# Gate projections by seven products of half blocks in a hybrid decoder layer, with tokens and gates parked in DRAM

## The reference

```python
h = rms_norm(x, norm1_g)
q, k, v, u, vs, ga, gb = split(h @ w_in)           # 512, 128, 128, 512, 512, 1024, 1024 columns
u  = gelu(u);  vs = layer_norm(gelu(vs))
oa = attention(q, k, v)                            # sliding window with sinks, 512 wide
ob = u * (causal_spatial(w_spatial) @ vs + b)      # 512 wide
h2 = sigmoid(ga) * (oa @ w_branch_a) + sigmoid(gb) * (ob @ w_branch_b)
x  = x + h2 @ w_out
x  = x + hier_moe(rms_norm(x, norm2_g))            # 16 experts of 256, top 2 of one group
```

## Time and profile before

| | |
|---|---|
| median of 3 runs | 940.69 us (940.2 to 943.37) |
| the profiled execution | 940.68 us, of which 938.9 us are the span of the trace |
| PE busy | 902.6 us (96%) |
| DVE, ACT, POOL busy | 459.1, 357.7, 226.6 us |
| mean DMA rate over the span | 126 GB/s |

### The profile page before, as it was taken

One profiled execution on the slowest core, in us unless ns is written; L12 is line 12 of the kernel. 1 busy time (PEld: TensorE's weight loads), 2 busy tenths in 40 slices (PEclk: granted clock), 3 DMA queues, 4 the chain that ended last, 5 costly groups with the idle time before them and its releaser, 6 DMA issues. The chain is left out here.

```text
span 938.9 us, 16170 instructions
## 1 busy us (share of the span) xinstructions
PE 902.6 (96%) x5389; PEld 808.4 (86%) x5390; DVE 459.1 (49%) x828; ACT 357.7 (38%) x623; POOL 226.6 (24%) x242
## 2 busy tenths in 40 slices
PE   8999999999999999999999999999889999999994
PEld 7777776787999999999999999999788888888883
DVE  5677876433222222222222236543887768577561
ACT  5666655210232112111121132221536667577561
POOL 2434221345220000000000011000043356354562
PEclk9999999999999999999999999999899999999998
DMA  7321310200302201101001006874539898989833
GB/s 248 113 68 47 123 51 22 72 0 1 104 1 68 68 34 42 59 34 66 34 34 67 22 25 208 315 263 124 176 102 305 289 321 275 320 261 314 276 54 45
DMA packets 57359, 118.57 MB, mean 126 GB/s; under 512 B 7469, under 2 KB 32749, under 8 KB 57296
## 3 DMA queue, kind: packets, MB, share of 16 engines
q1 hardware_dynamic: 49824, 100.10, 30.8%
q0 software_dynamic: 7488, 17.85, 8.5%
HBM read 105.37 MB, written 23.00 MB: 137 GB/s over the span
## 5 line engine op out<-in xcount | busy, mean ns | idle before, releaser
L1408 ACT ACTIVATE gate<-psum 128x352 f32<-128x352 f32 x48 | 22.4, 466 | 209.9 <-PE psum L79 209.7
L77 PE MATMUL psum<-w_hi,hT_hi 128*128 128x512 f32 (+3 forms) x224 | 83.0, 370 | 3.6 <-issue 1.9
L2193 DVE TENSOR_TENSOR hT_lo<-room,hT_hi (+1 forms) x32 | 72.1, 2291 | 17.2 <-ACT hT_hi L1881 17.2
L77 PE MATMUL psum<-hT_hi,x_xT_hi 128*128 (+1 forms) x192 | 77.8, 405 | 1.4 <-DVE x_xT_lo L2348 0.8
L78 PE MATMUL psum<-w_lo,hT_hi 128*128 128x512 f32 (+3 forms) x224 | 78.9, 352 | 0.0
L79 PE MATMUL psum<-w_hi,hT_lo 128*128 128x512 f32 (+3 forms) x224 | 78.8, 352 | 0.0
L77 PE MATMUL psum<-hT_hi,w_hi 128*128 128x352 f32 x240 | 77.4, 323 | 0.0
L78 PE MATMUL psum<-hT_lo,w_hi 128*128 128x352 f32 x240 | 76.9, 321 | 0.0
L79 PE MATMUL psum<-hT_hi,w_lo 128*128 128x352 f32 x240 | 76.9, 320 | 0.0
L78 PE MATMUL psum<-hT_lo,x_xT_hi 128*128 (+1 forms) x192 | 75.7, 394 | 0.0
L79 PE MATMUL psum<-hT_hi,x_xT_lo 128*128 (+1 forms) x192 | 75.6, 394 | 0.0
(11 more groups left out here) (353 smaller groups left out, 2306.3 us busy)
## 6 DMA issues: line engine op xcount, KB each, us to landing
room<-in_w_gu SPq DMA_DIRECT2D x16, 2048.0 KB
dn_raw<-in_w_dn SPq DMA_DIRECT2D x16, 1024.0 KB
g_w_raw<-in_w_ab SPq DMA_DIRECT2D x15, 768.0 KB, 4.3
xT_chunk<-in_xT SPq DMA_DIRECT2D x8, 528.0 KB, 3.7
x_in<-in_x SPq DMA_DIRECT2D x8, 512.0 KB, 3.5
out_y<-y SPq DMA_DIRECT2D x8, 512.0 KB, 3.4
hn_rows<-squares SPq DMA_DIRECT2D x8, 512.0 KB, 3.2
o_w_raw<-in_w_out_t SPq DMA_DIRECT2D x7, 512.0 KB, 6.8
```

The costliest lines, as they stand in the source:

```text
L77: eng.matmul(out, lh, rh, start=first and k == 0, stop=False)
L1408: act.activation(gate[:, (ab + c) % 2, :], bank(psum, gate_pair(ab, c))[:, 0:TC], ACT.Sigmoid).then_inc(gated.sem, 1)
L2193: dve.tensor_tensor(gu_lo[:, buf, ks], gu_raw[:, buf, ks], gu_hi[:, buf, ks].bitcast(F32), ALU.subtract).then_inc(gu_lo_made.sem, 1)
```

## The change

The two block programs `sgu_gate_phase` and `gates_phase` become one, `dense_phase`, whose loops are all written out.

**Gates.** Features are cut in two halves (k), tokens in two halves of 528 (HALF, taken as two pieces HC of 264), and output columns in two halves; a turn takes 128 columns of each half of the columns of one gate. Where eight block products of four chunks each stood, seven stand, of sums of blocks: A are blocks of weights, S1 to S4 sums of them, B blocks of h, T1 to T4 sums of those. There are eight turns, and 56 products of 24 matmuls of 264 columns. Their results are added by DVE out of PSUM in a chain (e1, u2, u3, out), and the sigmoids of the four blocks of the result are written by ACT in place and stored to DRAM.

**Sums of tokens.** `attention_phase` stores each scaled tile of h to DRAM, and h_scale waits until the store of the tile before has landed. It also stores oaT at its end, since the sums T1 and T2 take its place. In the opening the tokens come back as blocks, and DVE makes the sums and their low parts, ACT their high parts.

**u.** The last quarter of u is taken in four pieces of 264 columns, the far tokens first. The low half of ob is made by DVE (`ob_low`) and no longer by POOL. **Branches.** After all gates come the sixteen branch products (b, then a), with oaT and the sigmoids loaded back; POOL adds the two branches, and all eight chunks of h2 are split in this block. The first 18 matmuls of the output product (FIRST_K = 2 chunks) stand at the end of this block too.

```diff
@@ attention_phase, SP and DVE
+            def store_h(t):
+                sp.wait_ge(h_scaled, 2 * (t + 1))
+                sp.dma_start(io["h"][:, :, toks(t)], h_raw[:, :, :, 0:rows(t)]...).then_inc(h_stored, DMA)
+            store_h(0)
             for t in range(2, NT):
                 load_x(t)
                 load_xT(t)
+                if t >= 3:
+                    store_h(t - 2)
...
+            sp.wait_ge(oa_lo_made, NT)
+            for o, name in zip(oaT, ("oa_hi", "oa_lo")):
+                sp.dma_start(io[name], o[:, :, :]...).then_inc(oa_stored, DMA)
...
                 dve.wait_ge(h_lo_made, 2 * t)
+                dve.wait_ge(h_stored, DMA * t)
@@ dense_phase
+    UNITS = [(q, slice(c * TC, (c + 1) * TC)) for q in range(KE - 1) for c in range(3)]
+    UNITS += [(KE - 1, slice(c * HC, (c + 1) * HC)) for c in (2, 3, 0, 1)]
+    SUMS = ("A11", "S2", "S3", "A12", "S1", "A22", "S4")
+    SLOTS = 5
+        MOVING = (quarter(0, 0), T[2], T[3], quarter(1, 0), T[1], T[4], quarter(1, 1))
+        X_BANKS = (0, 1, 5, 6, 7, 2, 3, 4)
...
+        def _(sp):
+            load_u(1)
+            load_tokens(0, T_raw[1], 0, 1)
+            load_tokens(1, T_lent[3], 1, 1)
+            load_tokens(2, T_lent[1], 0, 0)
+            load_u(2)
             for used in keep["used"]:
                 sp.sem_clear(used)
...
+        def _(pool):
+            for v in range(KD, BRANCHES - 1):
+                pool.wait_ge(multiplied, 3 * v + 3)
+                pool.tensor_tensor(here, here, part[v % 2], ALU.add).then_inc(h2_summed, 1)
...
+        def _(act):
+            def gates(g):
+                n, i = divmod(g, len(SUMS))
+                for c in range(2):
+                    if i == 0:
+                        act.activation(e1[:, c], x_of(g, c), ACT.Copy).then_inc(e1_made, 1)
+                    elif i >= SUMS.index("A12"):
+                        act.wait_ge(x_taken, taken(g, c))
+                        act.activation(ready, ready, ACT.Sigmoid).then_inc(sg_made, 1)
...
+            for g in range(GATES):
+                gates(g)
+                if g in (0, 1):
+                    t_high(4, g)
+                high(g + SLOTS - 1)
...
+        def _(pe):
+            def gate_product(g):
+                pe.wait_ge(w_hi, g + 1)
+                pe.wait_ge(w_lo, g + 1)
+                for c in range(2):
+                    pe.wait_ge(x_taken, taken(g - 4, c))          # from g = 4 on
+                    product(pe, x_of(g, c), ..., KH).then_inc(m_made, 1)
...
+        def _(dve):
+            for u in range(US):
+                if u in (0, 3, 6):
+                    u_low(u // 3 + 1)
+                u_step(u)                                         # ob_low(u - 1), then the product with mixT
+                if u in (1, 2):
+                    first_sums(u - 1)
+                if u in (3, 4):
+                    second_sum(u - 3)
+                if u in (5, 6, 7):
+                    n = (1, 3, 2)[u - 5]
+                    for piece in range(2):
+                        t_low(n, piece)
+                if u == US - 4:
+                    low(0)
+                if u == US - 3:
+                    for name in ("S1", "S2", "S3"):
+                        weight_sum(0, name)
+                if u == US - 2:
+                    low(1)
+                    fourth_sum(0)
+            low(2)
+            ob_low(US - 1)
+            low(3)
+            fourth_sum(1)
+            weight_sum(0, "S4")
+            for g in range(GATES):
+                gates(g)
+                if g in (0, 1):
+                    t_low(4, g)
+                elif n + 1 < TURNS:
+                    for name in {2: ("S1",), 3: ("S2", "S3"), 4: ("S4",)}.get(i, ()):
+                        weight_sum(n + 1, name)
+                low(g + SLOTS - 1)
```

More of the change, by code:

```diff
@@ L37 @@
 TC = NTOK // 3
-EARLY = ((0,), (1,), ())
-LATE = sum(len(ks) for ks in EARLY)
+HALF = NTOK // 2
+HC = HALF // 2
+FIRST_K = 2
+ARENA = SG * NTOK + 4 * KD * P + 2 * (KD // 2) * HALF + 4 * TC + 2 * (KD // 2) * P
 NG, EPG = 4, 4
@@ L93, in u_bank @@
     return bank(psum, 2 + c)
-def gate_pair(ab, c):
-    return 2 * ((3 * ab + c) % 4)
 class Step:
@@ L310, in _ @@
             load_xT(1)
+            def store_h(t):
+                sp.wait_ge(h_scaled, 2 * (t + 1))
+                sp.dma_start(io["h"][:, :, toks(t)], h_raw[:, :, :, 0:rows(t)].rearrange("p a k c -> p (a k) c")).then_inc(h_stored, DMA)
+            store_h(0)
             for t in range(2, NT):
@@ L326, in _ @@
             load_vs(1)
+            store_h(PT - 1)
             sp.wait_ge(h_scaled, 2 * NT)
             sp.dma_start(kT_cache[:, :], io["cache_kT"]).then_inc(k_cache_in, DMA)
+            store_h(PT)
             sp.wait_ge(h_lo_made, 2 * NT)
+            sp.wait_ge(h_stored, DMA * NT)
             load_vs(3)
@@ L362, in _ @@
             sp.wait_ge(vs_stored, DMA)
+            sp.wait_ge(oa_stored, 2 * DMA)
         @block.gpsimd
@@ L1520, in merge_moe_phase @@
     hT, ident, y = (keep["hT_hi"], keep["hT_lo"]), keep["ident"], keep["y"]
-    h2 = keep["h2"]
     gu_flat, dn_raw = keep["gu_raw"], keep["dn_raw"]
@@ L1872, in keep_y @@
                 ins.then_inc(y_copied, 1)
-            for k in range(LATE, KD):
-                act.activation(hT[0][:, k, :], h2[:, k, :], ACT.Copy).then_inc(h2_hi, 1)
             for f in (gu_hi_made, dn_hi_made, xT_hi_made, silu_made, hidT_hi_made, out_made):
@@ L2023, in logits_turn @@
                 mm.then_inc(lg_turned, 1)
-            for k in range(KD):
-                wait(pe, h2_lo, k - LATE + 1)
+            for k in range(FIRST_K, KD):
                 for c in range(3):
-                    mm = term(0, c, k, k == 0, k == KD - 1)
+                    mm = term(0, c, k, False, k == KD - 1)
                     if k == KD - 1:
@@ L2197, in _ @@
                 f.begin(dve)
-            for k in range(LATE, KD):
-                dve.wait_ge(h2_hi, k - LATE + 1)
-                dve.tensor_tensor(hT[1][:, k, :], h2[:, k, :], hT[0][:, k, :].bitcast(F32), ALU.subtract).then_inc(h2_lo, 1)
             dve.memset(y[:, PT, :], 0.0).then_inc(zeroed, 1)
+            weights(1)
             dve.wait_ge(const_in, DMA * 4)
             dve.tensor_tensor(w_r, w_r, g2[:, :].unsqueeze(2).broadcast_to([P, KD, NR]), ALU.mult).then_inc(w_r_made, 1)
-            weights(1)
             dve.wait_ge(made, 3)
@@ L2429, in hybrid_layer @@
         with ExitStack() as dense:
+            with ExitStack() as short:
+                for name in ("hT_hi", "hT_lo"):
+                    keep[name + "_raw"] = sb(short, name + "_raw", [P, KD, NTOK])
             for name in ("hT_hi", "hT_lo"):
@@ L2432, in hybrid_layer @@
             with ExitStack() as branches:
+                with ExitStack() as short:
+                    for name in ("oaT_hi", "oaT_lo"):
+                        keep[name + "_raw"] = sb(short, name + "_raw", [P, KE * NTOK])
                 for name in ("oaT_hi", "oaT_lo"):
```

706 lines of the change are left out of this document (423 added, 283 removed).

## The result

The changed kernel takes **924.82 us** in the median (924.2 to 926.06, four runs), the kernel before beside it 940.6 us (940.2 to 943.37, four runs): a ratio of 0.9828, with a 95% interval of 0.9806 to 0.985. Faster, by 15.8 us, as forecast; 928.7 us had been predicted, within 924 to 934, so the time lies 0.8 us above the range's lower end. The span of its profiled execution is 923.6 us, against 938.9.

The account below looks back on a forecast made before the run. PE, at work 96% of the span, was taken as the bound. 23.9 us gained less 11.9 given back takes the 938.9 us span to 926.9; with execution's extra 1.8 that is 928.7 us, range 924 to 934.

Parts of the forecast that it names:

- The matrix work, -17.8: PE's matmuls from u to the output product: 320.5 us before, 302.8 after, with 264 columns 122.8 ns apart.
- Rival 4: Narrow matmuls don't pay: at 136 ns or more for 264 columns the gates gain nothing, 947 us; chance 0.03.
- rival 5: The change doesn't do what it says: halves refetched or PE's written-out code arriving late, 942 us; chance 0.04.
- The gates in their steady state, nothing: Gate turns: 19 us of DVE and ACT chain hidden beside 20.6 us of PE, costed at nothing.
- rival 1: Gates: the round DVE, ACT, DVE outlasts PE's 2.95 us a product; 948 us at 3.3 us; chance 0.13.
- The opening, 4.6 and 1.5 for the clock: First gate products: PE waits 4.6 us for DVE's low parts, plus 1.5 us for one lowered clock.
- The opening's loads: Block start: u weights and token blocks land in time at 390 GB/s, so PE doesn't wait for them.
- Attention, 2.4: h_scale of tile 2 waits for tile 1's store, landing at 33.6 us; 2.4 us lost, bounds 0.5 and 5.
- Branches, 0.5: Branch products: DVE beside POOL's adds lags by 3.5 us at most, costing PE 0.5 us.
- The end, 1.3 and 1.6 for the clock: Block's end: PE idles 1.3 us behind DVE's 4.1 us tail, and the lowered clock costs 1.6 us as before.
- Rival 2: The opening costs nothing: DVE and ACT keep up and no clock falls, 922.6 us; chance 0.14.

Follow-up runs that it names:

- the run in quarters: The kernel before with its gated feed-forward in four pieces of 264 columns in place of three of 352, all eight products kept: 946.58 us, ratio 1.0066.

## Why the prediction came out as it did

The mechanism was right: PE's work fell, PE waited in the opening but not in the turns, and attention lost by its store. Two groups of terms were mis-sized, of opposite sign, and part of the nearness in time is luck. By the predicted sum the stretch between the marks would have been 302.8 + 9.5 = 312.3 us; it was 305.1, so 7.2 better. Attention was 2.8 worse, the block's start and what follows the block 1.0. 926.9 - 7.2 + 2.8 + 1.0 = 923.5; the span is 923.6. Of the 7.2, the spacing gave 1.7, the opening 4.4, the branches 0.2 and the end 1.8, together 8.1. About 1.0 us of the stretch is neither matmuls at their spacing nor one of the three idle places; such a rest of 0.8 us stood there before too, and the prediction had counted it as gained.

- **The matrix work, -17.8.** With 121.6 ns at 264 columns in place of 122.8 it is 1,440 x 0.0012 = 1.7 more, -19.5 us. The line through the two measured widths was right to 1%. Rival 4 is refuted by it, and for rival 5 nothing speaks: no idle place in the block is one in which PE's own instructions came late. The rule of the Trainium skill, "TensorE: Matmul & The Clock Gate", section "Back-to-back issue gap", by an estimate from whose figures this change would have lost nearly 6 us, doesn't agree with these fp32r matmuls: neither here nor in the run in quarters did narrower ones come at its spacing.
- **The gates in their steady state, nothing.** Right. In 300 to 450 us PE is busy all the time, and no wait stands in turns two to seven. In that stretch DVE waits 24.6 us for PE (33 times) and 29.9 for ACT's high parts (30 times, mostly 1.01 us). The tripled low parts show that rival 1's mechanism exists, and that its margin was about 0.9 us a product, more than the 0.25 us that the sum had left (2.7 against 2.95).
- **The opening, 4.6 and 1.5 for the clock.** 1.68 us, with the clock at 1.00 behind. The step that failed is the walk along DVE. DVE's timeline before the wait:

```profile
285.38 2.08 DVE L1630 TENSOR_TENSOR arena<-arena 128x512 f32<-128x512 f32 x3
287.38 0.43 DVE L1588 TENSOR_TENSOR w_lo<-arena,w_hi 128x264 fp32r<-128x264 f32 x1
287.73 0.43 DVE L1583 TENSOR_TENSOR arena<-arena,mixT 128x264 f32<-128x264 f32 x1
289.17 0.69 DVE L1640 TENSOR_TENSOR w_lo<-arena,w_hi 128x512 fp32r<-128x512 f32 x1 [1.01 <-ACT w_hi L1443]
289.78 1.25 DVE L1618 TENSOR_TENSOR hT_lo_raw<-hT_hi_raw,oaT_hi 128x1056 f32<-128x1056 f32 x1
...
294.02 0.69 DVE L1640 TENSOR_TENSOR arena_rounded<-arena,arena_rounded 128x512 fp32r<-128x512 f32 x1 [1.01 <-ACT arena_rounded L1443]
```

  An instruction of DVE shown as 0.43 us is followed by the next after 0.35 (287.38 to 287.73), one of 0.69 after 0.61 (289.17 to 289.78): their ends overlap the next start by 0.08 us, when nothing is waited for. I had added up the durations. Over the more than twenty DVE instructions of the opening that follow another at once, that is close to 2 us. A handover took less too, 0.03 us (DVE's product ends at 288.16, ACT starts at 288.19; ACT ends at 289.14, DVE starts at 289.17), and I had taken 0.1. No run separates the two. The effect: low(1), forecast 1.9 us late, ended at 289.86 as PE came for it, and low(2) (294.02 + 0.69 = 294.71) was 1.7 late instead of a further 2.4 behind. The page names ACT's w_hi as the releaser; the time of the wait's end shows that it was this low part. Moving a sum behind it moved the wait whole, which fits that it is the sum of DVE's and ACT's work up to there. POOL's share in it was as costed: with it back, 0.6 us, and 1.01 us in place of 0.52, as in the earlier trace rows.
- **The opening's loads.** No wait of PE, as walked.
- **Attention, 2.4.** 5.24. The chain of waits was the one forecast (store, h_scale, exponentials, L754); only the landing was wrong, 35.9 in place of 33.6. Of that, 0.7 us is my choice: the sum gave 34.3, and no row supports the step down to 33.6. For the rest, I had taken 390 GB/s from the earlier trace rows, a stretch of weight loads; among attention's own DMAs it was 205 to 344, and the next load of x joined at 32.16. To this came the clock, 0.54 for 3 us behind 3.83 us of idling, which I had costed in the opening and at the end but not here. The kernels with the store ahead of the loads start the block at 237.7 us in the mean, as before the change: the order was the whole loss. (5.24 is one execution's; with the same order the others lost 3.6 to 6.1.)
- **Branches, 0.5.** PE lost 0.30 us there, but by another way: the store of c22, not POOL beside DVE. POOL's adds took 3.40 us beside DVE, as the 2.9 and the contention suggest, and DVE's products out of PSUM stayed at 0.53, while low parts of 512 columns took 2.95 in place of 0.69; the lag never reached PE. What the Trainium skill says in "SBUF — State Buffer", section "Who interferes with whom", agrees with this trace: 1.93 us for one DVE sum with two SBUF inputs beside POOL's add (541.54), 0.52 without.
- **The end, 1.3 and 1.6 for the clock.** 1.06, and no fall of the clock. Windows of PE behind both idle places:

```profile
294.00:297.00 3.00, 2.19 (x18) 1.00 0.00 0
297.00:300.00 3.00, 3.00 (x27) 1.00 0.00 0
548.00:551.00 3.00, 2.32 (x15) 1.00 0.46 93
551.00:553.00 2.00, 2.00 (x15) 1.00 0.99 386
```

  I had carried the 1.5 us from an idle place of 2.08 us to shorter ones. In the runs with a longer tail the clock fell at this place, behind 2.74 and 6.09 us.

Rival 2 (the opening costs nothing, 922.6) came close in time, but not in its cause: the opening still cost 1.7 us, and attention cost more.

## What to carry to other kernels

When a chain on VectorE is walked to see who comes late, use distances between starts of busy neighbours, not durations; 0.08 us each adds up to the wait in dispute. When a change adds a wait for a store, look first at what stands ahead of the store in its DMA queue: here the place of one store cost about 5 us of a gain of 21, and no engine's busy time shows it. Fewer matmuls at a narrower width are worth the difference of counts times spacing at each width, and both spacings are to be read from the same kind of matmul.

## What the runs showed of the hardware that was not expected

- fp32r matmuls of 264 columns came 121.5 ns apart, next to 159.0 at 352 and 119.5 at 256. From 256 to 264 the step is 2 ns, less than the 3.3 that 0.41 ns a column gives; the figure at 256 rests on 21 matmuls and is good to half a nanosecond.
- The length of one idle place of PE doesn't tell whether the granted clock falls. Places of 1.06, 1.68, 1.82 and 2.21 us left it at 1.00; places of 2.08 us in the kernel before, and of 2.74, 3.83, 6.09 and 6.21 us, had 3 to 7 us at the 1.2 GHz level around or behind them. But it fell as well at the start of the block in every profile, behind some 1.20 us (1.40 in the kernel before and its variant) with 0.98 us of idling some 2 us earlier. And one and the same place in the routing, 2.00 us before 655.93 in the changed kernel and 1.99 us before 655.88 in the run with the fourth sum moved, had a fall in the one and none in the other, with the same work around it. PE in the windows behind it, first the changed kernel:

```profile
656.00:659.00 3.00, 3.00 (x15) 0.51 0.99 289
```

```profile
656.00:659.00 3.00, 3.00 (x28) 1.00 0.97 288
```

  So a term for the clock behind a short idle place is a chance and not a sum; what decides it stays open.
- A store of one tile of h landed 7.2 us after its issue while weights and tokens were loaded beside it.
